# Four edits to a two-block transformer kernel on one core: turn to the expert stage, its end, the second block's order, and block norms by halves

## The reference

```python
def first_block(x, ...):
    h = rmsnorm(x, norm_mix)
    ...                                    # two kinds of attention, gates, w_out
    x = x + merged @ w_out
    h = rmsnorm(x, norm_ffn)
    x = x + (silu(h @ w_gate) * (h @ w_up)) @ w_down
    return rmsnorm(x, norm_final)

def second_block(x, ...):
    h = _rmsnorm(x, norm1_g)
    p = h @ w_in                           # q (512), k (128), v (128), conv a (512), conv gate (512)
    q, k = axial_rope(rmsnorm(q)), axial_rope(rmsnorm(k))
    attn_out = softmax(q k^T / 8) v        # all 256 keys, 8 heads, 2 key heads
    c = a * sigmoid(gate)
    c = depthwise_conv(c, 31 taps along the tokens) + b
    conv_out = silu(layernorm(c))
    x = x + concat(attn_out, conv_out) @ w_out
    x = x + peer(_rmsnorm(x, norm2_g))
    return _rmsnorm(x, final_g)

def peer(xc):                              # per token, 8 heads
    q = xc @ peer_wq
    s1, s2 = q[:128] @ keys[0].T, q[128:] @ keys[1].T
    # 16 best of each, 16 best of the 256 sums -> 16 of 16384 experts e, softmax g
    h = gelu(xc . peer_u[e])               # 16 rows of 1024 each
    return sum over heads and 16 of g * h * peer_v[e]
```

## Time and profile before

| | us |
|---|---|
| median of 3 runs | 1312.83 (1311.0 to 1312.92) |
| the profiled execution | 1310.15 |
| its span in the trace | 1308.3 |
| PE busy | 1059.4 (81%) |
| DVE busy | 725.4 (55%) |
| ACT busy | 408.5 (31%) |
| POOL busy | 901.7 (69%) |
| DMA | 356.97 MB, 268.47 of them by POOL's gathers |

### The profile page before, as it was taken

The page is one execution under the profiler, slowest core; times in us unless marked ns, Lnnn a source line. Parts: engine busy times, 40 slices in busy tenths (PEclk is TensorE's granted clock), DMA queues, the critical chain, the costliest instruction groups (busy, mean ns, idle before and its releaser), DMA issues. The chain is left out here.

```text
span 1308.3 us, 15510 instructions
## 1 busy us (share of the span) xinstructions
PE 1059.4 (81%) x5312; PEld 737.4 (56%) x5312; DVE 725.4 (55%) x1651; ACT 408.5 (31%) x711; POOL 901.7 (69%) x849
## 2 busy tenths in 40 slices
PE   5999989999999878989776776777767777767777
PEld 5989879899988876789622222222222232222222
DVE  3435323221161598649677656676567638677443
ACT  4345444444433524354322220222202220122202
POOL 5864437688889658547477777777777776777741
PEclk9999979999999979899999999999999999999999
DMA  6533223445545332035699999999999999999994
GB/s 231 192 133 126 97 97 129 160 180 191 186 171 194 127 129 97 2 115 200 209 411 409 409 409 410 410 410 410 409 410 409 409 409 409 409 409 409 410 409 167
DMA packets 86893, 356.97 MB, mean 273 GB/s; under 512 B 9649, under 2 KB 9777, under 8 KB 76721
## 3 DMA queue, kind: packets, MB, share of 16 engines
q0 software_dynamic: 73728, 268.47, 51.7%
q1 hardware_dynamic: 12672, 86.15, 18.5%
q10 hardware_dynamic: 432, 1.57, 0.3%
HBM read 355.10 MB, written 1.05 MB: 272 GB/s over the span
## 5 line engine op out<-in xcount | busy, mean ns | idle before, releaser
L919 PE MATMUL bank<-v_row,diag 128*128 128x512 f32 x1000 | 468.8, 613 | 183.8 <-DMA v_row<-peer_v_dram,expert 182.2
L1809 POOL TENSOR_TENSOR w_lo<-raw,w_hi 128x512 fp32r<-128x512 f32 x300 | 385.1, 1317 | 187.7 <-ACT w_hi L1010 187.2
L919 PEld LDWEIGHTS bank<-v_row,diag 128*128 128x128 f32 x1000 | 183.0, 192 | 469.4 <-issue 317.8
L1721 DVE CUSTOM_DVE_ANT_0 u_row<-u_row,bank 128x1024 f32<-128x1024 f32 x256 | 299.2, 1218 | 181.5 <-DMA u_row<-peer_u_dram,expert 179.4
L1847 POOL DMA_INDIRECT u_row<-peer_u_dram,expert x256 | 247.2, 966 | 98.4 <-issue 72.3
L1847 POOL DMA_INDIRECT v_row<-peer_v_dram,expert x256 | 240.5, 939 | 91.7 <-issue 73.5
L580 PE MATMUL bank<-hT_hi,w_hi 128*128 128x256 f32 x672 | 192.3, 286 | 4.1 <-DVE hT_lo L1294 4.1
L581 PE MATMUL bank<-hT_lo,w_hi 128*128 128x256 f32 x672 | 190.8, 284 | 0.0
L582 PE MATMUL bank<-hT_hi,w_lo 128*128 128x256 f32 x672 | 190.7, 284 | 0.0
L1010 ACT ACTIVATE w_hi<-raw 128x2048 fp32r<-128x2048 f32 x79 | 150.8, 1910 | 111.9 <-PE bank L582 111.9
L1208 ACT ACTIVATE gelu<-dots 128x16 f32<-128x16 f32 x16 | 3.5, 216 | 501.8 <-DVE dots L1721 501.8
(11 more groups left out here) (233 smaller groups left out, 1355.7 us busy)
## 6 DMA issues: line engine op xcount, KB each, us to landing
raw<-stream_dram SPq DMA_DIRECT2D x79, 1024.0 KB, 4.8
u_row<-peer_u_dram,expert POOLq DMA_INDIRECT x256, 14.4
v_row<-peer_v_dram,expert POOLq DMA_INDIRECT x256, 15.0
residual<-x_in_dram SPq DMA_DIRECT2D x2, 512.0 KB, 5.0
out_dram<-residual SPq DMA_DIRECT2D x4, 256.0 KB, 2.1
consts<-consts_in_dram SPq DMA_DIRECT2D x1, 840.0 KB, 9.8
gain<-norm_final_dram ACTq DMA_DIRECT2D x1, 512.0 KB, 5.4
gain<-norm_g_dram ACTq DMA_DIRECT2D x1, 512.0 KB, 3.7
```

Source lines behind the costliest of these rows:

```text
L919: ins = mm(accs[half][:, :], diag[:, 2 * m + i, :], row[:, half * 512:(half + 1) * 512], start=False, stop=True, skip_group_check=True)
L1721: ins = v.tensor_tensor_reduce(out=row_of_u, in0=row_of_u, in1=hn_tile[t][:, :], scale=1.0, scalar=0.0, op0=ALU.mult, op1=ALU.add, accum_o ...
L1809: ins = nc.gpsimd.tensor_tensor(w_lo[r][:, cols], raw[r][:, cols], w_hi[r][:, cols].bitcast(F32), ALU.subtract)
```

## The change

Four groups of edits.

*Norms by halves.* ACT squares each half of 512 columns when DVE has added it, adds the mean of the first half and EPS in the bias of the root, and DVE makes no sum or variance any more; `xs` is made and waited for in halves. In norm 2 ACT does this for X and hn both.

*Order of the second block.* conv0, conv1, kv, q20, q21, conv2, conv3, with banks given by hand; DVE's taps keep their running sum in PSUM (banks 2 and 0) and only the last tap of a channel group writes `conv_a`; they are handed out 8, 8, 6, 6, 4, 4 and then 6 a step; both q2 tiles are turned before attention; PE's taps are three a step from step 1 on; group 0 leads by 8 taps; POOL's taps come ahead of all splits of wp; two bridges are shorter.

*Turn to the expert stage.* POOL makes `hn`; DVE copies it to `hn_tile` after the first choice; the first choice reads the scores in their bank; the u buffers of batches 6 and 7 move to raw buffers 1 and 2 and wait for the second and third late split; two late splits come ahead of the first dot products; the second group's u rows are all asked for before the first v row, and only the v rows wait for the last query.

*End of the expert stage.* The last group's v rows go into the u buffers, as DVE's dot products free them; DVE adds batches 2, 4 and 6 and the first row of 7, PE the last row, with a semaphore of its own, half by half; the final squares follow by halves.

```diff
+FIRST_TAPS = (1, 3)
+TAP_BANK = (2, 0)
-SHARE = (2, 4, 6)
+SHARE = (2, 4, 6, 7)
-            + [f"conv{c}" for c in range(CC)] + ["kv", "q20", "q21"] + [f"wp{q}" for q in range(4)]
+            + ["conv0", "conv1", "kv", "q20", "q21", "conv2", "conv3"] + [f"wp{q}" for q in range(4)]
-BRIDGE = {0: 0, 1: 8, 2: 20, 3: 8, "mean": 22, "branch": 8}
+BRIDGE = {0: 0, 1: 8, 2: 14, 3: 8, "mean": 10, "branch": 8}
...
-    for c in range(CC):
-        ps.plan("D", ("conv", c))
+    for c in range(2):
+        ps.plan(None, ("conv", c), bank=c)
     for t in range(TT):
-        ps.plan("D", ("kv2", t))
+        ps.plan(None, ("kv2", t), bank=3 + t)
     for t in range(TT):
-        ps.plan("D", ("q2", t))
+        ps.plan(None, ("q2", t), bank=t)
+    for c in range(2, CC):
+        ps.plan(None, ("conv", c), bank=1 + c)
...
-        u_cols = [m0 + i * D for i in range(2 * EARLY_U)] + [x0 + 4 * D + i * D for i in range(2 * (BATCHES - EARLY_U))]
+        u_cols = [m0 + i * D for i in range(2 * EARLY_U)] + [GRAIN + i * D for i in range(2 * (BATCHES - EARLY_U))]
+        v_cols = [0, D] + [RING * GRAIN + i * D for i in range(2 * BATCHES - 4)] + [x0 + 4 * D, x0 + 5 * D]
...
                 for half in range(2):
                     for t in range(TT):
-                        if half == 0:
-                            pe.wait_ge(normed, TT * i + t + 1)
+                        pe.wait_ge(normed, 2 * TT * i + 2 * t + half + 1)
...
             g = TT * NH - 1
             pe.wait_ge(diag_done, 4 * (g + 1))
-            for m in range(BATCHES):
-                if m == BATCHES - 1:
+            for m in range(BATCHES - 1):
+                if m not in SHARE:
+                    pe.wait_ge(u_in[m], (g + 2) * PAIR_IN)
+                    add_rows(accs, m, rows_of(u_rows, m))
+            pe.wait_ge(last_in, 16)
+            for half in range(2):
+                cols = slice(half * 512, (half + 1) * 512)
+                mm(accs[half][:, :], diag[:, ETOP - 1, :], u_rows[ETOP - 1][:, cols], start=False, stop=True, skip_group_check=True)
+                if half == 0:
                     pe.wait_ge(share_done, 1)
...
+            def square(source, t, half, n):
+
+                settle(activation(full[:, 2 * t + half, :], source, ACT.Square, accum_out=sumsq[:, half, n:n + 1]))
+
+            def first_part(n):
+
+                settle(activation(column(var, n), sumsq[:, 0, n:n + 1], ACT.Copy, scale=1.0 / D, bias=EPS))
+
+            def root_of_sums(n):
+
+                activation(column(root, n), sumsq[:, 1, n:n + 1], ACT.Sqrt, scale=1.0 / D,
+                           bias=column(var, n)).then_inc(root_done, 1)
...
+            gate_of_conv(2)
+            gate_of_conv(3)
+            warm(ACT.Exp)
+            prepare("conv3", RING)
...
-                        ins = next_tap(v, conv_a[:, c, :], tap, c)
+                        ins = next_tap(v, conv_a[:, c, :] if tap == TAPS - 1 else acc(c), acc(c), tap, c)
...
-                        conv_taps(4)
+                        conv_taps(6)
...
-            dve.wait_ge(gain2_done, 16)
-            for t in range(TT):
-                v.tensor_tensor(hn[:, t, :], xs[:, t, :], gain2[:, :], ALU.mult)
-            for t in range(TT):
-                ps.copied(dve, ("norm", 3, t, 1))
-            settle(v.tensor_tensor(hn_tile[0][:, :], xs[:, 0, :], gain2[:, :], ALU.mult))
...
             choose(0, 0)
+            for t in range(TT):
+                ps.copied(dve, ("norm", 3, t, 1))
+            settle(v.tensor_copy(hn_tile[0][:, :], hn[:, 0, :]))
             late_split(NGRAN - 4)
             choose(1, 1)
             late_split(NGRAN - 3)
+            late_split(NGRAN - 2)
             dot_products(0, 0, range(0, 2))
-            late_split(NGRAN - 2)
-            dot_products(0, 0, range(2, 4))
             late_split(NGRAN - 1)
-            dot_products(0, 0, range(4, BATCHES))
+            dot_products(0, 0, range(2, BATCHES))
...
+            pool.wait_ge(gain2_done, 16)
+            for t in range(TT):
+                pool.wait_ge(normed, 2 * TT * len(TURNED) - 2 * TT + 2 * t + 2)
+                nc.gpsimd.tensor_tensor(hn[:, t, :], xs[:, t, :], gain2[:, :], ALU.mult).then_inc(hn_done, 1)
+            for n in range(NGRAN - LATE - 2, NGRAN - LATE):
+                low_part(n, n % RING)
...
             pool.wait_ge(experts_ready, 1)
             for m in range(BATCHES):
-                if m == EARLY_U:
-                    ps.full(pool, ("query", NH - 1))
+                if m >= EARLY_U:
+
+                    pool.wait_ge(late_split_done, LATE - RING + 1 + m - EARLY_U)
                 fetch_u(0, m, m + 1)
 
             pool.wait_ge(experts_ready, 2)
             for m in range(BATCHES):
                 fetch_u(1, m, BATCHES + m + 1)
+            ps.full(pool, ("query", NH - 1))
+            for m in range(BATCHES):
                 gather(peer_v, v_rows, v_in, 0, m)
...
             g = TT * NH - 1
             for m in range(BATCHES):
-                fetch_v(g % 3, m, (g - 1) * BATCHES + m + 1)
+                pool.wait_ge(u_free, (g + 1) * BATCHES + m + 1)
+                gather(peer_v, u_rows, u_in, g % 3, m, last_in if m == BATCHES - 1 else None)
```

More of the change, by code:

```diff
@@ L214, in gate_beside, with halves_in_order @@
     return None
+def halves_in_order(name):
+    halves = [(t, half) for t in range(TT) for half in range(2)]
+    return halves if name in (None, "down") else sorted(halves, key=lambda x: x[1])
 def nkeys(kind, t):
@@ L246, in attention @@
                 ps.plan("T", ("y", kind, 0))
+            if kind == "G" and s == FIRST_TAPS[0]:
+                ps.plan(None, ("taps",), bank=1)
         ps.plan("T", ("y", kind, 1))
@@ L1137, in _, with gate_of_conv @@
             high_of_norm(2)
-            for c in range(CC):
+            def gate_of_conv(c):
                 prepare(f"conv{c}")
@@ L1295, in low_of_norm, with residual @@
                                          hT_hi[where].bitcast(F32), ALU.subtract), name)
-            def residual(i, name, then=None):
-                halves = [(t, half) for t in range(TT) for half in range(2)]
-                if name != "down":
-                    halves.sort(key=lambda x: x[1])
-                for t, half in halves:
+            def residual(name, then=None):
+                for t, half in halves_in_order(name):
                     bank = ps.full(dve, (name, t, half))
@@ L1524, in _ @@
             low_of_merged(KD - 1)
-            residual(0, "out")
+            residual("out")
             norm(1)
```

237 lines of the change are left out of this document (120 added, 117 removed).

## The result

The changed kernel takes 1280.38 us (median of four runs, 1279.96 to 1285.43) where the kernel before takes 1312.22 (median of four, 1311.0 to 1312.92): a ratio of 0.9767, 95% interval 0.9741 to 0.9793. The forecast was 1273.7 with a range of 1265 to 1289. The profiled run has a span of 1278.6 us, 29.7 less than the 1308.3 of before; the prediction's sum was 39.15. Some 9.5 us of it are missing, and the profile says where. Against the forecast's own 39 us of gain the measured 32 are nearly a fifth short; the time still lies inside the range.

A forecast was written before the change was run, and what follows sets the result against it. DMA gathers bound the expert stage, half the time; a serial chain paced by PE lies ahead. Seven savings sum to 39.15 us: 1271.0 from the profiled 1310.15, or 1273.7 against the 1312.83 median; range 1266 to 1281 (wider 1265 to 1289).

The forecast's parts named there:

- Order of the block, 21.5: Second block: reordered granules and cheap taps with sums in PSUM start scores and mean sooner; 21.5 us less.
- Norm 3, 1.15: Norm ahead of the queries and experts: working by halves, with the flag write, saves 1.15 us.
- Norm 2, 0.4: Second block's norm: tile 0 is through early; 0.4 us less, between 1.5 more and 2 less.
- Rival (2): Lower PE clock, two more stretches than counted, idle before norm 2's transposes and scores speaking for it: 1280.5 us; chance 0.12.
- The turn, 10.8: Turn to the expert stage: sooner first choice and gathers without the query wait; 10.8 us less, excluding norm 3's 1.15.
- Rival (5): Expert gathers: DVE's w_lo splits don't hold them, thirteenth goes out near 622; 3.7 us less, 1270; chance 0.03.
- Norm 0, 1.8: First norm: ACT no longer needs DVE, so the first granule is split some 1.8 us sooner; 1.8 us less.
- the end, 2.4: Behind the last landing: sums and squares by halves, ACT squaring one half; 2.4 us less, bounds 0 and 4.
- (1): Turn to experts: gathers still have a hole, the turn gives 2 us instead of 10.8; 1282.5 us; chance 0.13.
- (3): Second block: DVE taps cost the mean before, 0.77 us, so attention steps become DVE's; 1294 us; chance 0.07.
- (4): Second block: PSUM taps beside POOL cost what they did beside splits; at 1.44 us a tap, 1345 us; chance 0.03.
- (6): PE clock: the stretches at the lower clock mostly vanish with the gaps; below 1265 us; chance 0.03.

The follow-up runs named there:

- the bridged kernel: Changed kernel with dummy products in PE's gaps (norms 2 and 3, q2 turns, turned probabilities) and hn waiting for both tiles' scaling: 1274.1 us, ratio 0.971 to before.
- the kernel with twenty dummies: Changed kernel with 20 dummy products instead of 14 ahead of norm 2's transposes: 1410.97 us on a long chip, ratio 1.0118 to before.

## Why the prediction was right, and where it was off

The time fell inside the range, and partly by luck. By the table the block, norm 2 and norm 3 together came out 13.0 us short of the forecast, norm 0, norm 1 and the end 1.0; 2.9 more than forecast at the turn and 1.6 of chance in the first block set some of it off.

**Order of the block, 21.5: measured 17.2, shown by two ways** (after's trace, with conv0's 2.1 of clock counted at norm 2; the order alone 17.1). The taps are right: 0.41 and 0.46 were taken, 0.40 beside splits and 0.484 by group are there, and the sums in SBUF show the price of the other choice. The rule of the Trainium skill (SBUF — State Buffer, Who interferes with whom), by which a DVE instruction with two SBUF inputs contends with a GpSimd one that reads SBUF, holds here: 810 ns against 484. The 120 against 58 cycles of the Trainium skill's VectorE: DVE Perf Modes (The TRN2 errata) don't show: 0.40 in a bank, 0.40 with both in SBUF and POOL idle. The steps are right (3.83 for 3.9). The mis-sized term is the start of the scores: 46.2 us behind conv0's first product forecast, 49.0 measured with conv0 at the full clock. Of the 2.8, 1.1 is a wait for GpSimd's split of conv2 (472.30), which the forecast had at nothing: the sign "no PE gap over 1 us" just failed there. Most of the rest is ACT's. Its chain was listed correctly, but its third rounding ends at 488.68 and only then come the copy of kT, a turn that needs the bank this copy frees (4.29 of idle PE), and the copy of qT: 7.1 us from the end of conv3, for 5.5. The other 2.9, from scores to mean, is a wait of 0.72 for y, one of 0.78 for PT (the turned probabilities, which ACT copies) and the low clock of the first two steps (the piece is 0.7 shorter in the bridged kernel and 1.5 in the one trace whose clock held throughout); 1.5 of all this had been allowed for.

**Norm 3, 1.15: measured -4.25. This is the step that failed,** and the edit that fails it stands under the turn to the experts. Moving hn to GpSimd was costed as free for DVE, since GpSimd would only wait. But GpSimd starts the product of tile 0 (567.19, 2.53 us) just when DVE scales the last half of tile 1: that half, the longest of its line, took 2.57, against 0.48 alone, and ended at 570.00, 0.28 behind the product. Undoing the overlap brings 2.1 back. The Trainium skill (same section) says of the 2-port modes that whoever issues first blocks the other for its whole instruction; durations of 2.53 and 2.57 that end so close agree. The second part is the clock, which the forecast had at nothing here: 0.60 over 570 to 580, 2.36 for the granule and its wait, 9.02 for 6.66. As far as is known hn is not to blame for it: the clock fell with hn moved away too (8.53), and held with the norms by halves alone (6.68), at the same gap of 2.15 between the transposes. It fell in seven of eight traces with that gap unfilled and in none of three with it filled; why it held in the eighth is open. The third part is the halves themselves: 0.24 was won and not 1.15. So 0.24 less 2.13 less 2.36.

**Norm 2, 0.4: measured -0.70,** inside the bounds that were given (1.5 more to 2 less), and with the 2.1 where the clock fell 2.8 more, outside them. The forecast named the idle time there and charged no clock for it. Rival (2) had named this place and the idle ahead of the scores; a third, norm 3, it had not. That its 1280.5 is the time that came out is chance in part: the two stretches at the lower clock that were not counted cost 4.5 and not 6.8, and hn, the scores, the first block and the turn make up the rest in both directions.

**The turn, 10.8: measured 13.7.** The step was right in kind, the wait is gone and no hole is left. DVE's late splits held the gathers less than was drawn: three gathers took 1.71, 1.16 and 0.96 longer up to the thirteenth, for the 2.1 apiece and the waits assumed, so the thirteenth went out 19.06 behind the first and not 24.7. Rival (5) isn't borne out: the gathers beside a split did take 2.65 and 2.10, as the 3.06 in the earlier trace rows. That the 13.7 come from the closed hole is read from the two traces; what the single edits of the turn give of it was not measured on a chip like the first.

**Norm 0, 1.8: 1.26; norm 1, 1.1: 1.07; the end, 2.4: 1.97,** a DVE row of 1.30 more and a square of ACT less, as drawn. The 1.61 in the first block is chance, by the spread above. Rivals (1), (3), (4) and (6) didn't come: no hole, taps at 0.48, clock dips that stayed.

Of the signs named, the mean came at 532.42 for 525, the first experts at 593.51 for 581 and the thirteenth gather 29.0 sooner for 36: the lateness of the scores, of norm 3 and of both clocks, carried on to each. The last landing to the end took 12.18 for 11. Of the three signs against it, no tap came over 0.6; PE did wait for DVE in attention, 0.72, and GpSimd for dot products, 19.9 us in all and at most 3.3 at once, while the DMA engines kept at 409 GB/s or more from slice 20 to the last but one.

## What to carry to other kernels

Work that is moved to an idle engine is not free: list what the other engines do in just those microseconds, and whether both go through the same port; a wait on the last of their instructions costs nothing where the result is needed later, and gave 2.1 us back here. When edits make PE's inputs come in pieces, look at the gaps between the pieces as at the gap ahead of them: behind those of norm 2, of the scores and of norm 3 the clock fell, in most runs, to or towards the lower of its two levels, 1.2 GHz for 2.4, which cost 0.7 to 2.4 us each, and dummy products in the gaps kept it at the upper one. Cut both traces at the same instructions before asking what an edit was worth: those pieces repeated to 0.1 us where whole times differed by 100.

## What the runs showed of the hardware that was not expected

Chips differ in the expert stage, and with them what the change is worth: the changed kernel has a ratio of 0.977 on the first kind, and three kernels one edit away from it have ratios near 1.012 on a long chip. From the first gather to the end of the span, in us:

```
                          chips like the first       long chips
old turn and end           700.2, 700.0               789.3, 789.3
new turn and end           684.8, 685.5, 685.1        811.1 to 821.9 (seven traces)
```
Of the two old ones on a long chip, one has the last norm by halves. The last line includes the kernel with the query wait put back, and it is the longest (821.9): the closed hole is not what makes the new one lose. A large part of the loss lies behind the last gather: from its issue to the end 35 to 38 us with the new end, 18 to 19 with the old, where the first kind has 28.5 and 26.6. The mean granted clock of the whole span is 0.87 to 0.90 on the long chips and 0.97 to 0.98 on the first kind. On the long chips DVE stops within its choice of experts, between instructions that wait for none of the engines. Timeline of DVE in the kernel with twenty dummies; in after the same choice has no gap of this kind.
```profile
908.63 0.76 DVE L1733 TENSOR_TENSOR gain<-c_digit,consts 128x256 f32<-128x256 uint32 x2 [3.88 <-remote]
911.43 0.76 DVE L1736 TENSOR_TENSOR gain<-gain,s_idx 128x256 f32<-128x256 f32 x2 [2.04 <-issue]
```
"remote" is a source that the profile doesn't record. PE has such stops too (up to 16.3 us), and they begin with the full stream of gathers: from the first query product to the last matmul of the queries it takes 46 to 48 us where a hole leaves the DMA engines idle (order alone, norms alone, query wait back) and 61 to 70 where the stream is closed; on the first kind of chip 45.6 with the stream closed. GpSimd then waits for DVE's dots, 112.0 us in all with the new turn (twenty dummies) and 68.2 with the old (order alone). So on such chips the stops come together with the full stream of gathers; that the stream causes them is argued, not shown, and what of the new turn or end loses some 22 us or more there was not tried. Order and bridges, which lie ahead of the stage, keep their gain on both kinds.
